# Strassen's seven products for 21 quads of weight blocks, and one loop written out

## The reference

```
h = rms_norm(x, norm_w[0])
z = h @ w_in_ab                      # 4096 x 13312
qa, ka, va, qb, kb, vb, gate = split(z)
oa = global attention of 16 heads (4 key heads), RMS-normalised and rotated q and k
ob = neighbourhood attention of 16 heads, learned bias
x  = x + (concat(oa, ob) * silu(gate)) @ w_out_ab
h = rms_norm(x, norm_w[1])
z = h @ w_in_c                       # 4096 x 10240
oc = windowed attention of 32 heads (8 key heads), sink logit, distance bias
x  = x + (oc * silu(gate)) @ w_out_c
out = rms_norm(x, final_norm_w)
```

## Time and profile before

| | |
|---|---|
| median of 3 runs | 2813.32 us (2813.13 to 2814.18) |
| the profiled execution | 2814.37 us, its span 2812.6 us |
| TensorE busy | 2797.6 us (99%), 12681 matmuls |
| VectorE busy | 1687.7 us (60%) |
| ScalarE busy | 1347.7 us (48%) |
| DMA engines busy, mean | 72% (queues 1 and 10) |
| granted TensorE clock | 0.998 of full speed |

### The profile page before, as it was taken

The page is one execution under the profiler, slowest core; times in us unless marked ns, Lnnn a source line. Parts: engine busy times, 40 slices in busy tenths (PEclk is TensorE's granted clock), DMA queues, the critical chain, the costliest instruction groups (busy, mean ns, idle before and its releaser), DMA issues.

```text
span 2812.6 us, 37759 instructions
## 1 busy us (share of the span) xinstructions
PE 2797.6 (99%) x12681; PEld 2329.4 (83%) x12681; DVE 1687.7 (60%) x2103; ACT 1347.7 (48%) x1654; POOL 16.4 (1%) x14
## 2 busy tenths in 40 slices
PE   9999999999999999999999999999999999999998
PEld 7888888888888888888888888888888888888886
DVE  7766666556556555566665556666655666665554
ACT  6455455445444444444443445555544455543333
POOL 0000000000000000000000000000000000000000
PEclk9999999999999999999999999999999999999999
DMA  9777777777767777677777767777676777676665
GB/s 334 222 210 232 225 226 221 224 217 228 234 209 215 228 220 239 189 254 254 253 240 222 223 211 218 231 233 220 221 226 204 231 227 225 216 251 218 215 209 187
DMA packets 357923, 637.17 MB, mean 227 GB/s; under 512 B 25376, under 2 KB 79136, under 8 KB 357792
## 3 DMA queue, kind: packets, MB, share of 16 engines
q1 hardware_dynamic: 343824, 593.52, 67.7%
q10 hardware_dynamic: 13968, 41.95, 4.1%
HBM read 585.56 MB, written 49.81 MB: 226 GB/s over the span
## 4 chain that ended last, share of the span: by engine, by line
PE 99%; DMA 0%; issue 0%; DVE 0%; ACT 0%; POOLq 0%; POOL 0%; SPq 0%; DVEq 0%; ACTq 0%
PE proj L1098 32%; PE proj L1099 32%; PE proj L1100 32%; PE o_ps L1099 1%; PE o_ps L1098 1%; PE sc_ps L1100 1%; PE o_ps L1100 1%; PE sc_ps L1099 1%; PE sc_ps L1098 1%; DMA raw<-in_w_in_ab 0%; DVE w_lo L757 0%; DVE x_fin L1091 0%; ACT w_hi L637 0%; POOLq L268 0%; POOL rms L598 0%
## 5 line engine op out<-in xcount | busy, mean ns | idle before, releaser
L757 DVE TENSOR_TENSOR w_lo<-raw,w_hi 128x1024 fp32r<-128x1024 f32 x990 | 1208.5, 1221 | 856.7 <-ACT w_hi L637 850.5
L637 ACT ACTIVATE w_hi<-raw 128x1024 fp32r<-128x1024 f32 x990 | 1049.6, 1060 | 1148.6 <-PE proj L1100 1087.3
L1098 PE MATMUL proj<-w_hi,h_hi 128*128 128x512 f32 x2936 | 1143.4, 389 | 2.0 <-issue 1.5
L1099 PE MATMUL proj<-w_lo,h_hi 128*128 128x512 f32 x2936 | 1142.8, 389 | 0.0
L1100 PE MATMUL proj<-w_hi,h_lo 128*128 128x512 f32 x2936 | 1142.1, 389 | 0.0
L1100 PEld LDWEIGHTS proj<-w_hi,h_lo 128*128 128x128 f32 x2936 | 551.2, 188 | 114.9
L1098 PEld LDWEIGHTS proj<-w_hi,h_hi 128*128 128x128 f32 x2936 | 551.4, 188 | 114.5 <-issue 2.4
L1099 PEld LDWEIGHTS proj<-w_lo,h_hi 128*128 128x128 f32 x2936 | 551.4, 188 | 109.9
L1098 PE MATMUL proj<-w_hi,y_hi 128*128 128x512 f32 x1024 | 398.4, 389 | 0.0
L1099 PE MATMUL proj<-w_lo,y_hi 128*128 128x512 f32 x1024 | 398.4, 389 | 0.0
L1100 PE MATMUL proj<-w_hi,y_lo 128*128 128x512 f32 x1024 | 398.3, 389 | 0.0
(11 more groups left out here) (115 smaller groups left out, 975.5 us busy)
## 6 DMA issues: line engine op xcount, KB each, us to landing
raw<-in_w_in_ab SPq DMA_DIRECT2D x414, 512.0 KB, 4.4
raw<-in_w_in_c SPq DMA_DIRECT2D x320, 512.0 KB, 4.4
raw<-in_w_out_ab SPq DMA_DIRECT2D x128, 512.0 KB, 4.5
raw<-in_w_out_c SPq DMA_DIRECT2D x128, 512.0 KB, 4.5
head_turn<-head_stage SPq DMA_DIRECT2D x256, 96.0 KB, 1.9
head_land<-head_turn ACTq DMA_DIRECT2D x64, 384.0 KB, 5.5
landing<-group_turn ACTq DMA_DIRECT2D x31, 512.0 KB, 5.5
group_turn<-q_stage SPq DMA_DIRECT2D x64, 128.0 KB, 3.2
```

The costliest lines, as they stand in the source:

```text
L637: nc.scalar.activation(w_hi[:, slot], raw[:, slot], ACT.Copy).then_inc(hi_ready, 1)
L757: nc.vector.tensor_tensor(w_lo[:, slot], raw[:, slot], w_hi[:, slot].bitcast(F32), ALU.subtract) \
L1098: nc.tensor.matmul(dst, hi, r_hi, start=start, stop=False)
L1099: nc.tensor.matmul(dst, hi, r_lo, start=False, stop=False)
```

## The change

In 12 entries of the plan without attention, which stand for 13 pairs, a "quad" of four blocks is multiplied by Strassen's seven products (in Winograd's form) instead of eight; eight of the pairs have two quads, five have one: 21 quads. The plan's entries get `quads` (which blocks, at which place), `heads` (how many heads' results must be there) and `combine` (when the sums of the left side are made).

A quad takes the rows c1 and c2 of both groups, in the order (0, c1), (1, c1), (1, c2), (0, c2). The left side (tokens) needs four sums of activations; they are made once per stage by `make_sums` and split in high and low, into rows of `h` or `y` that are not in use. The right side (weights) needs four mixes, made by VectorE for each quad from the raw slots (`quad_lo`). Seven operands are split into high and low. Each is half a block of work for TensorE: two row tiles, one token tile, six matmuls. `op` counts operands now, a quad takes eight numbers (the last is skipped), and slots of `w_hi` and `w_lo` go by operand, those of `raw` by block.

The products go to `x11, x21, x12, x22` (the four `proj` banks) and to three further banks, `m1`, `m6` and `m7` (which shares a bank with attention's `o_ps`). After the last quad of a pair ScalarE copies `m1` (`copy_m1`) and VectorE adds the banks up (`fold`, seven adds of 128x512). Group 1's ordinary blocks start at `second_at`, behind five of the adds. In a pair with quads all of group 0 comes before them, so that it is drained there and not at step 30.

The loop of three rounds over two pairs becomes six entries of their own. The two `x1` pairs behind the first stay a loop, of two rounds.

```diff
+QUAD = 4
+OPS = 8
+FOLDS = 7
+REST1, REST2 = [0, 1, *range(4, KC // 2)], [0, 1, *range(6, KC // 2)]
+VG_QUADS = with_quads([*REST1[:9], (2, 3), *REST1[9:]], REST1)
+X1_QUADS = with_quads([*REST1[:11], (2, 3), *REST1[11:]], REST1)
+TWO_QUADS = with_quads([*REST2[:4], (2, 3), *REST2[4:9], (4, 5), *REST2[9:]], REST2)
+TWO_VG = with_quads([*REST2[:5], (2, 3), *REST2[5:10], (4, 5), *REST2[10:]], REST2)
+LAST_QUADS = with_quads([*REST2[:2], (2, 3), *REST2[2:7], (4, 5), *REST2[7:-2]], REST2[:-2],
+                        [(g, EARLY + c) for g in range(2) for c in range(LATE)])
...
-        (1, [Pair("in_ab", vg(0), "vg", "qk", "qk", v=1)]),
-        (3, [Pair("in_ab", qk(1), "qk", "B", "vg", batch=4), Pair("in_ab", vg(1), "vg", "qk", "qk", v=2)]),
+        (1, [Pair("in_ab", vg(0), "vg", "qk", "qk", v=1, quads=VG_QUADS, heads=16, combine=((5, "vg", 0, 2), (26, "vg", 1, 4)))]),
+        (1, [Pair("in_ab", qk(1), "qk", "B", "vg", batch=4)]),
+        (1, [Pair("in_ab", vg(1), "vg", "qk", "qk", v=2, quads=TWO_VG, heads=20)]),
+        (1, [Pair("in_ab", qk(2), "qk", "B", "vg", batch=5)]),
+        (1, [Pair("in_ab", vg(2), "vg", "qk", "qk", v=3, quads=TWO_VG, heads=24)]),
+        (1, [Pair("in_ab", qk(3), "qk", "B", "vg", batch=6)]),
+        (1, [Pair("in_ab", vg(3), "vg", "qk", "qk", v=4, quads=VG_QUADS, heads=28)]),
...
-        (3, [Pair("out_ab", out_cols(1), "x1", "h", "x1", x_batch=0)]),
-        (1, [Pair("in_c", kvc(0), "kv", "h", "x1", x_batch=3)]),
-        (1, [Pair("in_c", c(0), "qg", "k", "kv", v=5)]),
+        (1, [Pair("out_ab", out_cols(1), "x1", "h", "x1", x_batch=0, quads=X1_QUADS, heads=32,
+                  combine=((6, "x1", 0, 2), (26, "x1", 1, 4)))]),
+        (2, [Pair("out_ab", out_cols(2), "x1", "h", "x1", x_batch=1, quads=TWO_QUADS, heads=32)]),
+        (1, [Pair("in_c", kvc(0), "kv", "h", "x1", x_batch=3, quads=X1_QUADS, heads=32,
+                  combine=((3, "qg", 0, 2), (26, "qg", 1, 4)))]),
+        (1, [Pair("in_c", c(0), "qg", "k", "kv", v=5, quads=TWO_QUADS, heads=32)]),
...
-        (1, [Pair("in_c", c(4), "qg", "k", "kv", v=6)]),
+        (1, [Pair("in_c", c(4), "qg", "k", "kv", v=6, quads=TWO_QUADS, heads=48)]),
...
-        (2, [Pair("out_c", out_cols(1), "x2", "none", "x2")]),
-        (1, [Pair("out_c", out_cols(3), "x2", "none", "x2")]),
+        (1, [Pair("out_c", out_cols(1), "x2", "none", "x2", quads=X1_QUADS, heads=64,
+                  combine=((6, "x2", 0, 2), (26, "x2", 1, 4)))]),
+        (1, [Pair("out_c", out_cols(2), "x2", "none", "x2", quads=TWO_QUADS, heads=64)]),
+        (1, [Pair("out_c", out_cols(3), "x2", "none", "x2", quads=LAST_QUADS, heads=64)]),
...
+            def quad_hi(p, k, start, part):
+                n = p.o + p.op[start]
+                (mix, mix3), mixes_done = mix_of[p.out], QUAD * (p.quad_n + k)
+                b11, _, b22, b21 = (raw[:, (start + r) % RING] for r in range(QUAD))
...
+                if part == 2:
+                    act.wait_ge(mixed, mixes_done + 1)
+                    act.wait_ge(block_done, n + 2 - RING + 1)
+                    nc.scalar.activation(w_hi[:, (p.op[start] + 2) % RING], mix[:], ACT.Copy).then_inc(hi_ready, 1)
...
+            def copy_m1(p, b):
+                if p.quads and b == p.last_quad + 2:
+                    act.wait_ge(folded, p.folds)
+                    act.wait_ge(lo_ready, p.o + p.op[p.last_quad] + OPS)
+                    act.wait_ge(block_done, p.o + p.op[p.last_quad] + 1)
+                    nc.scalar.activation(folds_of(p)[0], m1[:], ACT.Copy).then_inc(m1_copied, 1)
...
+            def quad_lo(p, k, start, part):
...
+                if part == 0:
+                    lo(0, b11)
+                if part == 1:
+                    second = (start + 1) % RING
+                    dve.wait_ge(raw_loaded[second], 16 * (p.n * (NB // RING) + (start + 1) // RING + (second > 1)))
+                    dve.wait_ge(lo_ready, n + 1)
+                    minus(mix, b12, b11).then_inc(mixed, 1)
+                    lo(1, b22)
+                if part == 2:
+                    dve.wait_ge(mixed, mixes_done + 1)
+                    minus(mix3, b22, b12).then_inc(mixed, 1)
+                    lo(2, mix)
+                    dve.wait_ge(mixed, mixes_done + 2)
+                    dve.wait_ge(lo_ready, n + 3)
+                    minus(mix, b22, mix).then_inc(mixed, 1)
+                    lo(3, mix3)
+                if part == 3:
+                    lo(4, b21)
+                    dve.wait_ge(mixed, mixes_done + 3)
+                    dve.wait_ge(lo_ready, n + 5)
+                    minus(b21, b21, mix).then_inc(mixed, 1)
+                    lo(5, mix)
+                    dve.wait_ge(mixed, mixes_done + 4)
+                    lo(6, b21, 2)
+                    dve.wait_ge(lo_ready, n + OPS)
...
+            def fold(p, b):
...
+                if b == p.last_quad + QUAD:
+                    dve.wait_ge(m1_copied, p.pair_w + 1)
+                    dve.wait_ge(block_done, p.o + p.op[p.last_quad] + 6)
+                    add(f2, m6[:], f1)
+                    dve.wait_ge(folded, p.folds + 1)
+                    add(f3, m7[:], f2)
+                if b == p.last_quad + QUAD + 1:
+                    dve.wait_ge(folded, p.folds + 2)
+                    add(f2, x22, f2)
+                    dve.wait_ge(folded, p.folds + 3)
+                    add(x22, x22, f3)
+                    add(x12, x12, f2)
+                if b == p.second_at:
+                    dve.wait_ge(block_done, p.o + p.op[p.second_at])
+                    add(x11, x11, f1)
+                    add(x21, x21, f3)
+                    dve.wait_ge(folded, p.folds + FOLDS)
...
                     for m, k in turns_at(p, b, 3):
                         split_turn(p, m, k)
...
+                    make_sums(p, b)
                     split_lo(p, b)
+                    if p.quads:
+                        fold(p, b)
...
+            def quad(p, k, start, part):
...
+                def times(r, left, dst, first, final, count=1):
+                    slot = (p.op[start] + r) % RING
+                    pe.wait_ge(lo_ready, n + r + 1)
+                    for j, (a_hi, a_lo) in enumerate(left):
+                        last = three_passes(dst[:], a_hi, a_lo, w_hi[:, slot, j], w_lo[:, slot, j],
+                                            first and j == 0, final and j == 1)
+                    last.then_inc(block_done, count)
...
+                if part == 0:
...
+                    times(0, of_tile(c1, 0), m1, opens, closes)
+                    times(1, of_sum(3), x12, opens, closes)
+                if part == 1:
+                    times(2, of_sum(0), x22, opens, closes)
+                    times(3, of_sum(2), m7, opens, closes)
+                if part == 2:
+                    times(4, of_tile(c2, 0), x11, False, False)
+                    times(5, of_sum(1), m6, opens, closes)
+                if part == 3:
+                    times(6, of_tile(c2, 1), x21, False, False, 2)
```

More of the change, by code:

```diff
@@ L119, with __init__ @@
 class Pair:
[L128 removed]
+    def __init__(self, w, cols, out, side, before, batch=None, x_batch=None, v=None, quads=None,
+                 heads=0, heads_step=0, combine=()):
         self.w, self.cols, self.out, self.side, self.before = w, cols, out, side, before
@@ L193, in plan @@
         n += rounds * len(pairs)
+        ops += rounds * pairs[0].o_step
+        quads += rounds * pairs[0].quad_step
+        folds += rounds * pairs[0].folds_step
         x += rounds * x_step
@@ L643, in drain @@
+            def drain(p, g, out):
+                act.wait_ge(block_done, p.o + p.op[p.done0] if g == 0 else p.o)
+                if g == 0 and p.quads:
+                    act.wait_ge(folded, p.folds + FOLDS)
                 for t in range(TT):
```

281 lines of the change are left out of this document (232 added, 49 removed).

## The result

The changed kernel takes 2838.89 us (median of 4 runs, 2836.25 to 2840.76). The kernel before, on the same chip, takes 2813.62 us (4 runs, 2813.13 to 2814.18). The ratio is 1.0089, 95% interval 1.0072 to 1.0107: 25.3 us slower. I had forecast 2825.0, 11.7 slower. So the direction and the range (2803 to 2840) held, and the loss is more than twice the forecast.

A forecast was written before the change was run, and what follows sets the result against it. TensorE, busy 99% of the span, was taken to bound the kernel. Terms -28.6 - 2.1 + 17.8 + 3.6 + 21.0 = +11.7 on the profiled 2814.37, less 1.05, gave 2825.0 us; range 2803 to 2840.

The forecast's parts named there:

- The gain, 30.7: On TensorE, 126 fewer matmuls save 28.6 us and the written-out loop's two turns save 2.1 us.
- The last quad's wait, 13 x 1.37: Block behind a pair's last quad: TensorE stalls 1.37 us because `copy_m1` precedes that block's copy; 17.8 us in all.
- the walk through one quad: Timed order of one quad's copies, low parts and mixes: first of two stalls nothing, last of a pair stalls 1.37 us.
- The folds, 3.6: Second group's first block waits for the fold's adds in the two `TWO_VG` pairs, 1.8 us each.
- VectorE's other work, 21.0: Squares, transposes, tile splits, `add_x2` and `make_sums` falling into quads stall TensorE 21 us, ends 0 to 31.
- the first two rivals: VectorE's other work is absorbed wholly (2804 us, chance 0.20) or half (2814 us, chance 0.13).
- SyncE's queue: Load for the block three behind a quad and stores of turns stay hidden: 0, ends to 0.7 us a quad (15).
- Loads are late: Rival: raw slots come free out of step with blocks, adding 0.7 us a quad, 2840 us; chance 0.07.
- Clock: Rival: stalls in three first quads drop TensorE to 1.2 GHz, 3 x 9.5 us more, 2854 us; chance 0.03.
- The products step as any other: Opposing rival: six matmuls in a row into one bank step wider, 9 us more, 2834 us; chance 0.02.

The follow-up runs named there:

- the run with half loads: The changed kernel with the loads of the quads' 84 blocks cut to their first row tile, 256 instead of 512 KB: 2825.25 us, ratio 1.0037.

## Why the prediction was right, and where it was wrong

**The gain, 30.7: right.** 126 matmuls fewer, and the turns gone.

**The last quad's wait, 13 x 1.37: right**, by the walk through one quad. The trace of the last quad of the `c(0)` pair (product 0 at 1676.8) has the walk's order and times: the copy of operand 6 at 5.4 (walk: 5.3), the copy of `m1` at 7.9 (7.7), the next block's at 8.4 (8.4):

```profile
1682.18 1.07 ACT L799 ACTIVATE w_hi<-raw 128x1024 fp32r<-128x1024 f32 x1 [1.31 <-DVE raw L952]
1684.69 0.60 ACT L807 ACTIVATE zb<-m 128x512 f32<-128x512 f32 x1 [1.44 <-DVE w_lo L952]
1685.18 4.32 ACT L766 ACTIVATE w_hi<-raw 128x1024 fp32r<-128x1024 f32 x4
```

I had taken the copy's length from a scaled one of the same size (0.684, L651); it is 0.60. Moving the copy showed that the mechanism is the one named.

In the other last quads this wait is up to 1.56, 19.3 in all.

**The folds, 3.6: right**, 1.75 twice.

**VectorE's other work, 21.0: right in sum** by the run with half loads (19.4), in part by luck. It was not absorbed, so the first two rivals fall. Its terms in that run: 3.4 for 4.2 in the first quads of the output pairs, 2.7 for 3.3 in the last pair's, 0.69 for 0.8 in the two `c` pairs. But the 0.6 for the third output pair of the second layer and the 0.9 for the first quads of `vg(1)` and `vg(2)` are 0 there (2.4 in all), and one term is missing from my list: the second quads of pairs wait 0.6 to 0.7 in three cases, before product 5 (2.0). The one-quad pairs have 6.2 for 5.2, 3.5 of it in `vg(0)`, where the copy of operand 1 is late in that run too.

**SyncE's queue, "Hidden", 0 us: this step failed.** I followed one load, that of the block three behind the quad, and the stores. I did not follow the four loads of the quad itself. Its third block is the second operand, so its copy is wanted 5.2 us before product 0 and no longer 2.5. The walk had the copy at -5.20 and nowhere asked when the load goes out. From rows that I had: the block two ahead of the quad is copied at -5.44 - 7.92 = -13.4, its low part ends at -11.0, and a load of 4.5 lands at -6.5. The trace has it so where nothing is in front: out at -10.9, landed at -6.5. That is 1.3 us of slack for this load, in a queue whose engines are busy 74% of the time. It is soon gone: the load for the quad at 1407.66 went out 4.9 us late, behind a landed tile, and the one for the quad at 931.8 went out 1.1 late and took 2.5 longer than the median. "ScalarE waits for such a load for 18.5 us in all before" was misread: 18.5 is the part of one weight tensor, `in_w_in_ab`, and the four together are 30.2. It was evidence about the old order of wants, too, not the new one; in the changed kernel the copies of ordinary blocks wait 86.2 us for loads and those of operand 1 another 41.4. The rival that came true is "Loads are late", with 15 us for its bound; the run with half loads gives it 8.4 in the profile and 14 in the medians. Its mechanism was not as I wrote it: freeing a slot behind a quad earlier gained nothing in the run that tried it; what costs is the lead that is missing ahead of the quad.

**The wider steps, 2.2 us,** were in no term: I gave each wait 0.14 for its restart and its follower and took the steps behind it as 0.2267. These 2.2, the 1.5 by which the last quads' waits are longer and the 6.8 inside quads, for which the loads' 8.4 more than account, are the difference between forecast and profiled execution.

**Clock: right.** The granted clock of the changed kernel is 0.999 over its span, and 1.00 in a stretch with three of the longest waits (span, busy per engine, granted clock, DMA share, GB/s, as the earlier trace rows); behind the end it is 0.71:

```profile
1372.00:1396.00 24.00, 20.80 (x89) 16.02 (x88) 22.25 (x34) 11.87 (x14) 0.00 (x0) 1.00 0.74 236
...
2824.00:2834.00 10.00, 0.00 (x0) 0.00 (x0) 3.83 (x9) 3.39 (x4) 0.93 (x1) 0.71 0.95 373
```

The first row also shows VectorE at 22.25 of 24 us: in that quad it is the bound. The Trainium skill (TensorE: Matmul & The Clock Gate, Why this matters for your kernels) has idle gaps between bursts of matmuls bring the half clock back. Waits of up to 1.9 us, three within 6, didn't do it here.

**The products step as any other** (0.2265 on the mean at the start of a quad, from 1407.66 to 1411.51), so that rival falls too.

**What stays open.** Kernels with many waits seem to scatter more: the changed one over 4.5 us in 4 runs, the early copy over 8.9 in 9, the loop written out over 1.2 in 10; but the kernel before, over 1 in its first 4, has 2.2 to 4.7 in the three groups of experiments. The loads vary enough to do it: of the same quad (product 0 at 1311.2 in the changed kernel) the copy of operand 1 comes at -4.1 there and at -2.3 both with the early copy and with the slot freed earlier, and the waits inside quads are 27.8, 29.9 and 34.2 us in these three traces. But one trace of each kernel doesn't tell scatter from what the edit does. So the late load's price is 8 by one pair of profiles and 14 by medians. How much of a load's 6 to 7 us is other traffic wasn't tried either.

## What to carry to other kernels

Where a low part or any other preparation is made per operand, a product saved on TensorE is paid in elementwise work: here 11 operations of 1.22 us for 9.5 us of matmuls. Count that first, and put such quads where the elementwise engine has nothing else to do; one quad late in each pair, with `m1` copied early, gains 12 us (2 to 3 of it the loop's), 21 quads lose 25.

When operands are taken in another order than their blocks arrive, write down for each block when its slot comes free, when its load goes out and when it is wanted; one block's time off the lead left 1.3 us here. Write down, too, what fills each engine's waits: putting an operation behind the one that the engine waits for, to give a load more time, took away the 1.1 us that it had cost nothing before. And a short instruction with a long wait belongs behind whatever the others need sooner: moving one copy of 0.60 us was worth 17 to 19.

## What the runs showed of the hardware

- Subtractions of 128x1024 on VectorE with no wait between them start 1.14 us apart, though each is recorded with 1.22 (1407.60, 1408.74 above); where one needs the result just made, 1.32 (1408.74, 1410.06).
- A copy of 128x512 from PSUM to SBUF on ScalarE without scaling takes 0.60 us, 13 times within 3 ns; the scaled one takes 0.684.
- Behind a wait TensorE's steps are wider for more than the first two matmuls: 0.232 on the mean of the next ten (1412.82 to 1415.14), against 0.2267.
- A 512 KB load lands after 4.4 or 4.5 us in the median of its tensor, but the 21 loads of `b22` in the changed kernel's trace took from 3.6 to 7.0 us.
